# Making the seeds of the matrix Q on GpSimd alone, where VectorE made those of one channel half

## The chip, the cores and the metric

The kernel runs on one core of a Trainium2 chip. The metric is the device time of one execution, in microseconds. The core has five engines with an instruction queue each: TensorE (PE, matrix products), VectorE (DVE) and ScalarE (ACT) for elementwise work, GpSimd (POOL), and SyncE (SP), which issues transfers. Every queue is worked through in order, and the engines wait for each other by semaphores that the program names.

## The reference

It is one layer of a hybrid trunk over 2048 tokens of 1024 channels in float32. What matters here is the token mixer. Beside a gated short convolution it has a recurrence with one 64x64 state per head, for 16 heads:

```python
def step(state, inp):
    r_t, w_t, k_t, v_t, kk_t, a_t = inp
    sa = jnp.einsum('bhvk,bhk->bhv', state, kk_t)
    state = (state * w_t[:, :, None, :]
             - sa[..., None] * (kk_t * a_t)[:, :, None, :]
             + v_t[..., None] * k_t[:, :, None, :])
    y = jnp.einsum('bhvk,bhk->bhv', state, r_t)
    return state, y
...
merged = jax.nn.sigmoid(ga) * y_conv + jax.nn.sigmoid(gb) * y_rwkv
return merged @ w_out, v_first
```

After the mixer come a router and 32 experts of which each token uses two, and a last RMSNorm.

## The kernel before

The mixer is worked out in 32 steps. A step takes one tile of 128 channels (two heads, called the two halves; `HALF[0]` is partitions 0 to 63, `HALF[1]` is 64 to 127) and one group of 512 tokens, which is eight chunks of 64 tokens (`NC` = 8, `C` = 64). In a step the recurrence inside a chunk is turned into matrix products. They need the inverse of a triangular 64x64 matrix for each of the 16 pairs of chunk and head. The kernel builds it by doubling: two matrices `Tm` and `Qm` per pair start from a near-diagonal seed and are improved over five levels.

TensorE's order in a step is a projection part (`head` and `tail`: 64 products of 128x512 at L892 and some others), and then `inverse_and_recurrence`. That part goes by a list written out by hand, `SCHED`, which interleaves the products for the inverse of step i with the hops of the recurrence of step i-1 (`x`, `u` and `sy` for each chunk). It begins so:

```text
L, x0, LT (first half), u0, LT (second half), sy0, GK (first half), x1, GK (second half), u1,
Z1, sy1, TR0, T1, x2, Q1, u2, Z2, sy2, TR1, x3, T2, u3, Q2, sy3, ...
```

On TensorE `L` is L998, `LT` L1000, `GK` L1002, every `Z` L1004, every `T` L1006, every `Q` L1017, and every `TR` (a turn of `vt`, `Bb` or `Kb`) L986. The hops are L921 and L924 (x), L933 and L935 (u), L949 to L961 (sy) and L909 (the first part of the next x). All of them stand in one queue. In it T1 waits for the evacuation of Z1 (`Zm`) and for the semaphore `Q_seeded`, which says that the seeds of `Qm` are complete.

VectorE takes the results out of PSUM in the order of the same list: `Tm` from L (L1848), `LTb` from LT and `GKb` from GK in two operations each (L1837, `evacuate`), then `Zm` from Z (L1848), `Tm` and `Qm` from T and Q (L1851). Between them stand the state updates `St` (L1691). Behind the second evacuation of LT it calls `half_seeds`: two operations (L1858) that multiply one half of `LTb` with the mask `m0Ts` and write partitions 64 to 127 of `Qm`. Each covers 64 partitions by 4 chunks by 64 columns, 64x256.

GpSimd has six operations in a step (`seeds`): it adds the identity to `Tm` (L659), makes the seeds of partitions 0 to 63 of `Qm` in two operations of 64x256 (L663), waits for VectorE's two by the semaphore `Q_half`, adds the identity to all of `Qm` (L668) and tells TensorE by `Q_seeded`. Behind that it scales `Bb` and `Kb` in place (L653, `hat`). Those are read by the turns TR2 to TR5, in levels 3 to 5.

Of the kernel before, what the change touches and what calls it, by code (L numbers as in the profile page):

```python
# [9 lines left out]
ALU = mybir.AluOpType  # L10
# [14 lines left out]
HD = 64  # L25
# [58 lines left out]
def build(nc, io, out):  # L84
    ctx = ExitStack()
    with ctx:
# [3 lines left out]
        var_done gup_done bonus_done proj_done sg_ready a_ready carry_saved ksq_ready norm_max rk_ready  # L90
        rkbd_ready kk_ready b_ready ch_copied u_carry u_made cb_gated x_done u_done s_done y_done x_copied
        x_begun x_ahead yT_summed Q_near u_copied S_updated S_init yT_copied merged_ready merged_out gram_done
        gram_evac T_seeded Q_half Q_seeded tok_copied wo_in bcast_rows mix_done mixed x1_ready xn2_ready
        logit_done logit_copied aff_ready rank_mm hot_ready idx_mm idx_ready dest_ready blk_ready gu_done
        sig_ready silu_ready act_ready actT_done actT_ready y2_done y_dve y12 x2_ready o_ready shift_scaled
        shifted operands gates branch km_step rn_step P_step hats rs_step yc_step post_step conv_step sumsq
        ln_done rstd tr_done T_act T_dve index_col chain patterns ada_trip pair_go""".split()
        S = {n: ctx.enter_context(nc.semaphore(n)) for n in names}
        by_slot = "ada_w x_in mT_in x5_in x1_out xn2_out wi_in wo_e_in xg_in y_out".split()
        SL = {n: [ctx.enter_context(nc.semaphore(f"{n}{s}")) for s in range(2)] for n in by_slot}  # L100
# [6 lines left out]
        def sb(stack, name, shape, dt=F32):  # L107
            return stack.enter_context(nc.sbuf_tensor(name, shape, dt))
# [27 lines left out]
        m0Ts = sb(ctx, "m0Ts", [P, HD])  # L136
# [58 lines left out]
        LTb = [sb(p4, f"LTb{x}", [P, NC, 2 * HD]) for x in range(2)]  # L195
        GKb = [sb(p4, f"GKb{x}", [P, NC, 2 * HD]) for x in range(2)]
        Tm = sb(p4, "Tm", [P, NC, HD])
        Qm = [sb(p4, f"Qm{x}", [P, NC, HD]) for x in range(2)]
# [156 lines left out]
        evac_at = {u: n for n, u in enumerate(ON_DVE)}  # L355
        tok_at = {u: n for n, u in enumerate(ON_ACT)}
        NDV, NTK = len(ON_DVE), len(ON_ACT)

        def wait_gram(eng, i, u):

            eng.wait_ge(S["gram_done"], i * NUSE + use_at[u] + 1)

        def wait_evac(eng, i, u):

            if u in evac_at:
                eng.wait_ge(S["gram_evac"], i * NDV + evac_at[u] + 1)
            else:
                eng.wait_ge(S["tok_copied"], i * NTK + tok_at[u] + 1)
# [7 lines left out]
        HALF = (slice(0, 64), slice(64, 128))  # L376
# [254 lines left out]
        def _(pool):  # L631
# [15 lines left out]
            def over8(m):  # L647
                return m.unsqueeze(1).to_broadcast([P, NC, HD])

            def hat(i, p, M, n):  # L650
                pool.wait_ge(S["operands"], i * 5 + 2)
                pool.wait_ge(S["operands"], i * 5 + n)
                nc.gpsimd.tensor_tensor(M[:, :, :], M[:, :, :],  # L653
                                        pcs[p][:, :].unsqueeze(2).to_broadcast([P, NC, HD]), ALU.mult)\
                    .then_inc(S["hats"], 1)

            def seeds(i, p):
                wait_evac(pool, i, ("L", 0, 1, 0))
                nc.gpsimd.tensor_tensor(Tm[:, :, :], Tm[:, :, :], over8(idents[:, :]), ALU.add).then_inc(S["T_seeded"], 1)  # L659
                wait_evac(pool, i, ("LT", 0, 0, 0))  # L660
                pool.wait_ge(S["T_seeded"], i + 1)
                for a in range(2):
                    nc.gpsimd.tensor_tensor(Qm[p][HALF[0], 4 * a:4 * a + 4, :], LTb[p][HALF[a], 0:4, HD:2 * HD],  # L663
                                            m0Ts[HALF[a], :].unsqueeze(1).to_broadcast([HD, 4, HD]), ALU.mult)\
                        .then_inc(S["Q_near"], 1)
                    pool.wait_ge(S["Q_near"], i * 2 + a + 1)
                pool.wait_ge(S["Q_half"], i + 1)
                nc.gpsimd.tensor_tensor(Qm[p][:, :, :], Qm[p][:, :, :], over8(idents[:, :]), ALU.add)\  # L668
                    .then_inc(S["Q_seeded"], 1)
                hat(i, p, Bb, 4)  # L670
                wait_gram(pool, i, ("GK", 0, 1, 0))
                hat(i, p, Kb, 5)

            seeds(0, 0)
            seeds(1, 1)
            with pool.Fori(1, STEPS // 2) as h:
                seeds(h * 2, 0)
                seeds(h * 2 + 1, 1)
# [864 lines left out]
        def _(dve):  # L1543
            V = nc.vector
# [195 lines left out]
            def step(i, p):  # L1740
# [93 lines left out]
                def evacuate(kind, lv, b):  # L1834
                    u = (kind, lv, b, 0)
                    wait_gram(dve, i, u)
                    V.tensor_tensor((LTb if kind == "LT" else GKb)[p][:, 4 * b:4 * b + 4, :],  # L1837
                                    bank(u)[:, :].rearrange("p (c t) -> p c t", t=P),
                                    over(mN[:, :], 4), ALU.mult).then_inc(S["gram_evac"], 1)

                def evacuate_both(kind, lv):
                    u = (kind, lv, 1, 0)
                    wait_gram(dve, i, u)
                    bk = DUO[pair_of(u)][:, :, 0:4 * HD].rearrange("p b (c t) -> p b c t", t=HD)
                    to = {"L": Tm, "Z": Zm, "T": Tm, "Q": Qm[p]}[kind][:, :, :].rearrange("p (b c) t -> p b c t", b=2)
                    if kind in ("L", "Z"):
                        mask = m0s[:, :] if kind == "L" else mlevs[:, lv - 1, :]
                        ins = V.tensor_tensor(to, bk, mask.unsqueeze(1).unsqueeze(1).to_broadcast([P, 2, 4, HD]),  # L1848
                                              ALU.mult)
                    else:  # L1850
                        ins = V.tensor_tensor(to, to, bk, ALU.subtract)  # L1851
                    ins.then_inc(S["gram_evac"], 2)

                def half_seeds():

                    dve.wait_ge(S["gram_evac"], i * NDV + evac_at["LT", 0, 1, 0] + 1)
                    for a in range(2):
                        ins = V.tensor_tensor(Qm[p][HALF[1], 4 * a:4 * a + 4, :], LTb[p][HALF[a], 4:8, HD:2 * HD],  # L1858
                                              m0Ts[HALF[a], :].unsqueeze(1).to_broadcast([HD, 4, HD]), ALU.mult)
                    ins.then_inc(S["Q_half"], 1)  # L1860

                def hop(name, c):
                    if q is not None and name == "sy":
                        S_update(q, c, 1 - p)

                done = None
                for n, (what, name, *more) in enumerate(SCHED):
                    if what == "use" and name != "TR" and 1 in more[1]:
                        if name not in ("LT", "GK"):
                            evacuate_both(name, more[0])  # L1870
                        else:
                            evacuate(name, more[0], 0)
                            if SCHED[n + 1][0] == "hop":
                                hop(*SCHED[n + 1][1:])
                                done = n + 1
                            evacuate(name, more[0], 1)
                            if name == "LT":
                                half_seeds()
                    if what == "hop" and n != done:
                        hop(name, more[0])  # L1880
                if q is not None:
                    y_sum(q)

            step(0, 0)
            step(1, 1)
            with dve.Fori(1, STEPS // 2) as h:
                step(h * 2, 0)
                step(h * 2 + 1, 1)
# [258 lines left out]
```

## Time and profile before

| What | Value |
| --- | --- |
| median of 3 runs | 4946.42 us (4941.43 to 4950.04) |
| time of the profiled execution | 4945.55 us |
| its span, first to last instruction | 4943.8 us |
| granted TensorE clock, mean | 0.973 |
| TensorE busy | 4566.7 us, 92% |
| VectorE busy | 1631.0 us, 33% |
| ScalarE busy | 1346.4 us, 27% |
| GpSimd busy | 345.4 us, 7% |

The span is what the trace covers; the time is some 1.8 us longer and is what the runs are compared by. The mixer's 32 steps lie between about 200 us and 3080 us of the span.

### The profile page before, as it was taken

The page shows a single profiled execution, that of the slowest core. Times are in us where ns is not written, and L with a number is a line of the kernel's source. Part 1 is how long each engine was busy: PE and PEld are TensorE (multiplying, and loading weights), DVE is VectorE, ACT ScalarE, POOL GpSimd, SP SyncE. Part 2 cuts the span into 40 slices and gives each one's busy share as a digit, 9 for nine tenths or more (in the row PEclk, how much of TensorE's full clock was granted, in tenths as well). Part 3 has the DMA queues.
Part 4 walks back from the last instruction along what each step waited for, and adds up shares of the span by engine and source line. Part 5 has one row for each costly group of instructions (what it writes and reads, how often), then busy time and mean ns, then how long its engine had stood idle before and what let it go on. Part 6 is the DMA issues. An engine that isn't in the chain of part 4 may idle for free.

```text
span 4943.8 us, 91839 instructions
## 1 busy us (share of the span) xinstructions
PE 4566.7 (92%) x36823; PEld 2450.1 (50%) x36823; DVE 1631.0 (33%) x2946; ACT 1346.4 (27%) x3050; POOL 345.4 (7%) x466
## 2 busy tenths in 40 slices
PE   6999999999999999999999998994999999999992
PEld 4455555555555555555555555453444444444440
DVE  3334334334334334333343343224111111111115
ACT  4123333333333333333333333431111111111115
POOL 0001001001001000000010000000000000000004
PEclk8999999999999999999999999996999999999996
DMA  8101001001001001001001002333788888888887
GB/s 295 50 5 47 11 8 47 10 12 43 10 12 43 10 12 45 9 12 46 8 12 46 8 12 69 107 123 132 281 330 334 339 330 341 333 330 343 331 321 297
DMA packets 252914, 637.61 MB, mean 129 GB/s; under 512 B 11027, under 2 KB 96245, under 8 KB 252533
## 3 DMA queue, kind: packets, MB, share of 16 engines
q1 hardware_dynamic: 238852, 582.26, 32.3%
q0 software_dynamic: 13680, 49.81, 2.6%
q8 instruction: 295, 4.83, 0.4%
q14 instruction: 87, 0.70, 0.0%
HBM read 563.32 MB, written 68.71 MB: 128 GB/s over the span
## 4 chain that ended last, share of the span: by engine, by line
PE 87%; issue 4%; DVE 3%; DMA 2%; ACT 1%; SPq 1%; POOL 0%; DVEq 0%; POOLq 0%; ACTq 0%
PE bank L892 36%; PE bank L1218 18%; PE bank L1237 9%; PE bank L1106 5%; PE duo L1017 3%; PE duo L1004 2%; PE duo L1006 1%; PE duo L1207 1%; DMA yb<-y_s,dix 1%; PE bank L949 1%; ACT xs L1264 1%; PE bank L933 1%; PE duo L829 1%; PE duo L986 1%; PE bank L921 1%
## 5 line engine op out<-in xcount | busy, mean ns | idle before, releaser
L892 PE MATMUL bank<-hT,w 128*128 (+1 forms) x4096 | 1788.3, 593 | 0.0
L892 PEld LDWEIGHTS bank<-hT,w 128*128 128x128 f32 x4096 | 776.3, 190 | 991.0 <-issue 991.0
L1218 PE MATMUL bank<-WI,xT 128*128 128x512 f32 x2016 | 877.6, 593 | 2.4 <-DVE xT L2055 2.4
L1218 PEld LDWEIGHTS bank<-WI,xT 128*128 128x128 f32 x2016 | 378.9, 190 | 456.1 <-issue 456.1
L1237 PE MATMUL bank<-WO,aT 128*128 128x512 f32 x1008 | 443.1, 592 | 1.0 <-DVE ysb L2072 1.0
L1264 ACT ACT_TABLE_LOAD x268 | 343.8, 1283 | 21.1 <-DVE ub L1807 14.3
L2061 DVE TENSOR_TENSOR gsig<-bank,gsig 128x512 f32<-128x512 f32 x63 | 43.6, 692 | 847.4 <-ACT gsig L1264 847.4
L1237 PEld LDWEIGHTS bank<-WO,aT 128*128 128x128 f32 x1008 | 186.7, 190 | 212.6 <-issue 211.4
L1264 ACT ACTIVATE gsig<-bank 128x512 f32<-128x512 f32 x63 | 37.6, 597 | 827.6 <-PE bank L1218 827.6
L659 POOL TENSOR_TENSOR Tm<-Tm,idents 128x512 f32<-128x512 f32 x32 | 40.6, 1269 | 2826.3 <-DVE Tm L1848 2826.3
L1106 PE MATMUL bank<-wo,mT 128*128 128x512 f32 x512 | 233.6, 603 | 0.0
L1017 PE MATMUL duo<-Qm,Zm 64*64 64x64 f32 x5120 | 195.3, 225 | 16.5 <-issue 9.1
L1017 PEld LDWEIGHTS duo<-Qm,Zm 64*64 64x64 f32 x5120 | 176.4, 139 | 25.9 <-issue 21.9
L1264 ACT ACTIVATE T<-bank,par 128x512 f32<-128x512 f32 x96 | 66.0, 688 | 417.0 <-PE bank L892 417.0
L2072 DVE TENSOR_TENSOR ysb<-bank,g2b 128x512 f32<-128x512 f32 x126 | 81.2, 686 | 287.5 <-PE bank L1237 287.5
L1851 DVE TENSOR_TENSOR Qm<-Qm,duo 128x512 f32<-128x512 f32 x160 | 110.1, 688 | 191.0 <-PE duo L1017 191.0
L1264 ACT ACTIVATE xs<-bank 64x64 f32<-64x64 f32 x496 | 107.9, 218 | 145.2 <-PE bank L924 142.4
L1004 PE MATMUL duo<-Tm,LTb 64*64 64x64 f32 x5120 | 126.8, 225 | 21.0 <-issue 20.6
L1106 PEld LDWEIGHTS bank<-wo,mT 128*128 128x128 f32 x512 | 93.9, 191 | 101.1 <-issue 99.6
L1264 ACT ACTIVATE aT<-duo 128x512 f32<-128x512 f32 x63 | 37.6, 597 | 389.6 <-PE duo L1227 389.6
L1851 DVE TENSOR_TENSOR Tm<-Tm,duo 128x512 f32<-128x512 f32 x128 | 88.0, 688 | 155.2 <-PE duo L1006 155.2
L1264 ACT ACTIVATE ut<-bank 64x64 f32<-64x64 f32 x496 | 81.3, 212 | 184.6 <-PE bank L935 184.6
(340 smaller groups left out, 5369.0 us busy)
## 6 DMA issues: line engine op xcount, KB each, us to landing
WI<-in_w_expert_in_dram SPq DMA_DIRECT2D x63, 4096.0 KB, 17.2
WO<-in_w_expert_out_dram SPq DMA_DIRECT2D x63, 2048.0 KB, 7.9
w<-in_w_in_dram SPq DMA_DIRECT2D x64, 512.0 KB, 3.9
y_s<-ysb SPq DMA_DIRECT2D x63, 512.0 KB, 17.8
adaw<-in_w_ada_dram SPq DMA_DIRECT2D x12, 2048.0 KB, 12.9
xt<-in_x_dram SPq DMA_DIRECT2D x16, 512.0 KB, 9.0
WAc<-rank_s SPq DMA_DIRECT2D x32, 256.0 KB, 3.4
GDc<-rank_s SPq DMA_DIRECT2D x32, 256.0 KB, 3.2
```

Source lines behind the costliest of these rows:

```text
L829: mm(SB[:, :], UP[0:64, 0, :], WAc[0:64, :], start=True, stop=True).then_inc(S["zdec_done"], 1)
L892: ins = mm(PJ[j % 2][:, :], w[:, j, k, :], hT[:, k, ds(group(i) * G, G)], start=k == 0, stop=k == KT - 1)
L921: mm(xb[a][HALF[a], 0:HD], GKb[p][HALF[a], 4 * a + k, HD:2 * HD], tok[p][HALF[a], 0, 2 * k + a, :], start=True, stop=False)
L933: mm(xb[h][ha, 0:HD], Qm[p][HALF[h], slot_of(c), :], xsb[HALF[h], :], start=True, stop=False)
L1004: ins = mm(one, LTb[p][rows, e, HD:2 * HD], Tm[rows, e, :], start=True, stop=True)
L1017: ins = mm(bks[b][hp, k * HD:k * HD + HD], Zm[hp, c, :], Qm[p][hp, c, :], start=True, stop=True)
L1106: ins = mm(banks[2 * s + j][:, :], mT[:, s, k, :], wo[:, k, j * 512:j * 512 + 512], start=k == 0, stop=k == KT - 1)
L1218: ins = mm(GU[j][:, :], xT[:, s, k, :], WI[:, s, k, j * DE:j * DE + DE], start=k == 0, stop=k == KT - 1)
L1237: ins = mm(Y2[j][:, :], aT[:, s, k * P:k * P + P], WO[:, s, k, j * 512:j * 512 + 512], start=k == 0, stop=k == DE // P - 1)
L1264: return nc.scalar.activation(o, i, f, **kw)
L1851: ins = V.tensor_tensor(to, to, bk, ALU.subtract)
L2072: ins = V.tensor_tensor(ysb[:, s, 512 * j:512 * j + 512], banks[2 + j][:, :], g2b[:, 512 * j:512 * j + 512], ALU.mult)
```

## The change

VectorE's `half_seeds` is taken out, with its semaphore `Q_half`. GpSimd makes the seeds of both halves, in four operations of 64x256 one behind the other, and for the second half it waits for the second evacuation of LT. The operations are the same, and so are their operands. All else stays.

```diff
             def seeds(i, p):
                 wait_evac(pool, i, ("L", 0, 1, 0))
                 nc.gpsimd.tensor_tensor(Tm[:, :, :], Tm[:, :, :], over8(idents[:, :]), ALU.add).then_inc(S["T_seeded"], 1)
-                wait_evac(pool, i, ("LT", 0, 0, 0))
                 pool.wait_ge(S["T_seeded"], i + 1)
-                for a in range(2):
-                    nc.gpsimd.tensor_tensor(Qm[p][HALF[0], 4 * a:4 * a + 4, :], LTb[p][HALF[a], 0:4, HD:2 * HD],
-                                            m0Ts[HALF[a], :].unsqueeze(1).to_broadcast([HD, 4, HD]), ALU.mult)\
-                        .then_inc(S["Q_near"], 1)
-                    pool.wait_ge(S["Q_near"], i * 2 + a + 1)
-                pool.wait_ge(S["Q_half"], i + 1)
+                for h in range(2):
+                    wait_evac(pool, i, ("LT", 0, h, 0))
+                    for a in range(2):
+                        nc.gpsimd.tensor_tensor(Qm[p][HALF[h], 4 * a:4 * a + 4, :],
+                                                LTb[p][HALF[a], 4 * h:4 * h + 4, HD:2 * HD],
+                                                m0Ts[HALF[a], :].unsqueeze(1).to_broadcast([HD, 4, HD]), ALU.mult)\
+                            .then_inc(S["Q_near"], 1)
+                        pool.wait_ge(S["Q_near"], i * 4 + 2 * h + a + 1)
                 nc.gpsimd.tensor_tensor(Qm[p][:, :, :], Qm[p][:, :, :], over8(idents[:, :]), ALU.add)\
                     .then_inc(S["Q_seeded"], 1)
...
-                def half_seeds():
-
-                    dve.wait_ge(S["gram_evac"], i * NDV + evac_at["LT", 0, 1, 0] + 1)
-                    for a in range(2):
-                        ins = V.tensor_tensor(Qm[p][HALF[1], 4 * a:4 * a + 4, :], LTb[p][HALF[a], 4:8, HD:2 * HD],
-                                              m0Ts[HALF[a], :].unsqueeze(1).to_broadcast([HD, 4, HD]), ALU.mult)
-                    ins.then_inc(S["Q_half"], 1)
-
...
                             evacuate(name, more[0], 1)
-                            if name == "LT":
-                                half_seeds()
```

## Rows read from the trace of the kernel before

**Rows 1.** The page: busy time, its share and the instructions of each engine.

```profile
PE 4566.7 (92%) x36823; PEld 2450.1 (50%) x36823; DVE 1631.0 (33%) x2946; ACT 1346.4 (27%) x3050; POOL 345.4 (7%) x466
```

**Rows 2.** Stretches of one step: length, busy time (and count) of PE, PEld, DVE, ACT, POOL; clock.

```profile
1391.97:1399.60 7.63, 6.42 (x201) 5.26 (x201) 6.54 (x12) 2.27 (x12) 4.84 (x5) 1.00 0.01 2
1399.60:1424.00 24.40, 20.34 (x632) 17.23 (x632) 10.23 (x20) 8.63 (x37) 1.35 (x2) 1.00 0.01 4
1424.00:1483.50 59.50, 59.49 (x140) 26.14 (x138) 19.19 (x34) 19.06 (x25) 0.00 (x0) 1.00 0.05 14
```

**Rows 3.** Timeline of the same step, TensorE: start, length, instructions, idle before.

```profile
1396.00 0.65 PE L1002 MATMUL duo<-AR,Kb 64*64 64x128 f32 x14
...
1397.08 0.69 PE L1004 MATMUL duo<-Tm,LTb 64*64 64x64 f32 x32
...
1398.30 0.28 PE L961 MATMUL bank<-AR,St 64*64 64x64 f32 x2
1399.00 0.41 PE L986 MATMUL duo<-ident,vt 128*128 128x128 f32 x2 [0.42 <-DVE GKb L1837]
1399.60 0.69 PE L1006 MATMUL duo<-Zm,Qm 64*64 64x64 f32 x32 [0.19 <-DVE Zm L1848]
```

**Rows 4.** Timeline of the same step, VectorE.

```profile
1395.52 0.69 DVE L1837 TENSOR_TENSOR LTb<-duo,mN 128x512 f32<-128x512 f32 x1
1396.24 1.29 DVE L1858 TENSOR_TENSOR Qm<-LTb,m0Ts 64x256 f32<-64x256 f32 x2
1397.57 1.29 DVE L1837 TENSOR_TENSOR GKb<-duo,mN 128x512 f32<-128x512 f32 x2
1398.77 0.68 DVE L1848 TENSOR_TENSOR Zm<-duo,mlevs 128x512 f32<-128x512 f32 x1
```

**Rows 5.** Timeline of the same step, GpSimd.

```profile
1395.52 1.73 POOL L663 TENSOR_TENSOR Qm<-LTb,m0Ts 64x256 f32<-64x256 f32 x2 [0.31 <-DVE LTb L1837]
1397.68 1.27 POOL L668 TENSOR_TENSOR Qm<-Qm,idents 128x512 f32<-128x512 f32 x1 [0.43 <-DVE Qm L1858]
1398.90 1.05 POOL L653 TENSOR_TENSOR Bb<-Bb,pcs 128x512 f32<-128x512 f32 x1
```

**Rows 6.** Timeline of the same step, the four seed operations one by one.

```profile
1395.52 0.73 POOL L663 TENSOR_TENSOR Qm<-LTb,m0Ts 64x256 f32<-64x256 f32 x1 [0.31 <-DVE LTb L1837]
1396.32 0.93 POOL L663 TENSOR_TENSOR Qm<-LTb,m0Ts 64x256 f32<-64x256 f32 x1
...
1396.24 0.42 DVE L1858 TENSOR_TENSOR Qm<-LTb,m0Ts 64x256 f32<-64x256 f32 x1
1396.68 0.86 DVE L1858 TENSOR_TENSOR Qm<-LTb,m0Ts 64x256 f32<-64x256 f32 x1
```

**Rows 7.** GpSimd's seeds over the whole run: durations in ns, least, median and longest.

```profile
L663 POOL TENSOR_TENSOR Qm<-LTb,m0Ts x64: 722/762/947, 216.8 to 3048.0; 64x256 f32<-64x256 f32 x64
```

**Rows 8.** Timeline of the first step, GpSimd and TensorE.

```profile
216.79 1.59 POOL L663 TENSOR_TENSOR Qm<-LTb,m0Ts 64x256 f32<-64x256 f32 x2
218.47 1.27 POOL L668 TENSOR_TENSOR Qm<-Qm,idents 128x512 f32<-128x512 f32 x1
...
219.87 0.53 PE L1006 MATMUL duo<-Zm,Qm 64*64 64x64 f32 x21 [0.19 <-POOL Qm L668]
```

**Rows 9.** Timeline of the last step, GpSimd and TensorE.

```profile
3049.27 1.26 POOL L668 TENSOR_TENSOR Qm<-Qm,idents 128x512 f32<-128x512 f32 x1 [0.43 <-DVE Qm L1858]
...
3052.64 0.69 PE L1002 MATMUL duo<-AR,Kb 64*64 64x128 f32 x3 [4.44 <-issue]
...
3055.95 1.13 PE L1006 MATMUL duo<-Zm,Qm 64*64 64x64 f32 x32
```

**Rows 10.** Waits of TensorE in 28 steps: in total, times, longest.

```profile
PE duo L1004 <- issue: 18.7, 25, 1.0
PE bank L935 <- issue: 14.4, 14, 1.3
...
PE duo L1006 <- issue: 8.2, 17, 0.7
...
PE duo L1017 <- issue: 5.7, 12, 0.9
```

**Rows 11.** Timeline of TensorE: Q1 in three steps of these twelve.

```profile
395.17 0.33 PE L1017 MATMUL duo<-Qm,Zm 64*64 64x64 f32 x4 [0.94 <-issue]
...
577.94 0.97 PE L1017 MATMUL duo<-Qm,Zm 64*64 64x64 f32 x26 [0.32 <-issue]
...
2779.19 0.62 PE L1017 MATMUL duo<-Qm,Zm 64*64 64x64 f32 x14 [0.68 <-issue]
```

More of the change, by code:

```diff
@@ L92, in build @@
         x_begun x_ahead yT_summed Q_near u_copied S_updated S_init yT_copied merged_ready merged_out gram_done
[L93 to L97, printed above, removed]
+        gram_evac T_seeded Q_seeded tok_copied wo_in bcast_rows mix_done mixed x1_ready xn2_ready logit_done
+        logit_copied aff_ready rank_mm hot_ready idx_mm idx_ready dest_ready blk_ready gu_done sig_ready
+        silu_ready act_ready actT_done actT_ready y2_done y_dve y12 x2_ready o_ready shift_scaled shifted
+        operands gates branch km_step rn_step P_step hats rs_step yc_step post_step conv_step sumsq ln_done
+        rstd tr_done T_act T_dve index_col chain patterns ada_trip pair_go""".split()
         S = {n: ctx.enter_context(nc.semaphore(n)) for n in names}
```

## The prediction

> **What bounds the kernel now.** I read the page first: TensorE is busy 92% of the span, VectorE 33%, GpSimd 7% [rows 1]. This says only that TensorE's queue sets the time. The busy time of another engine counts for nothing by itself; what counts is where TensorE waits for it. So next I read the stretches of one step, the one that begins near 1392 us (the 14th of 32). The reader is to see that TensorE has no slack in 59.50 us of it, 59.49 busy. Its idle time lies in the part that this change touches, 1.2 us of 7.63, and in the 24.40 us behind it [rows 2]. The change is made in VectorE's and GpSimd's queues, so its price in a step is how far it moves the first thing that TensorE waits for. TensorE doesn't catch up later: behind T1 everything stands in one queue, and the products of the inverse feed on each other.
>
> TensorE's timeline shows two such waits. TR0 waits 0.42 us for the evacuation of GK, and T1 starts at 1399.60, 0.15 after the end of `Zm` (1398.77 + 0.68 = 1399.45) [rows 3, 4]. The second condition of T1, the complete seeds of `Qm`, is met at 1397.68 + 1.27 = 1398.95 [rows 5]. It has 0.50 us of slack. So VectorE's chain ends last before T1, and GpSimd's chain is right behind it.
>
> **What the change removes.** VectorE loses two operations of 64x256, from 1396.24 to 1397.53. They are followed by GKb at 1397.57 and Zm at 1398.77 [rows 4]. Without them GKb can start when the product GK ends, 1396.65 [rows 3], and some 0.1 us for the signal, say 1396.75. Two evacuations of 1.29 us end at 1398.04. Zm comes behind both them and the product Z1 (ends 1397.77 [rows 3]); I let it start at 1398.0 and end at 1398.7. So `Zm` is 0.75 us earlier. TR0 starts as soon as the queue is through with sy1, whose last products end at 1398.58 [rows 3]. T1 starts 0.60 behind TR0 [rows 3], so TensorE could then have T1 at about 1399.1 to 1399.2, 0.4 to 0.5 us sooner. Removal alone would be a gain of 0.4 to 0.5 us a step.
>
> **What it adds.** GpSimd gets two more operations of 64x256 in front of the identity. The first of the present two runs beside a VectorE evacuation and takes 0.73; the second starts 0.80 after the first and takes 0.93, because it lies beside VectorE's seeds, which are 0.42 and then 0.86 long [rows 6]. The two engines stretch each other there: each has one short and one long operation, and the short ones are the free durations. With VectorE's seeds gone, what runs beside GpSimd's are evacuations from PSUM. Those cost it nothing in the rows: the first seed beside LTb takes 0.73, and the identity beside GKb takes the 1.27 that it takes in the first step too [rows 5, 6, 8]. So I take 0.73 for all four, which is also near the least of all 64 (722 ns) [rows 7], and 0.80 from start to start.
>
> The Trainium skill bears on this (SBUF — State Buffer, section "SBUF: two separate sides"): a VectorE operation with two SBUF inputs and a GpSimd operation that reads SBUF take a shared pair of ports in turns, each for a whole instruction. This case's trace agrees, with 0.86 against 0.42. By this rule the second to fourth seed take 0.73; without it one might leave them at 0.93, and the term below would be 0.6 us larger in a step.
>
> The chain in the step near 1392 us is then: seeds at 1395.52, 1396.32, 1397.12 and 1397.92; the second evacuation of LT ends at 1396.21 [rows 4], so the third seed doesn't wait. Identity at 1398.72, done at 1398.72 + 1.27 = 1399.99. That is 1.04 later than before. T1 starts 0.13 to 0.15 behind what it waits for (0.13 behind GpSimd in the first step: 218.47 + 1.27 = 219.74, T1 at 219.87 [rows 8]), so at 1400.14 instead of 1399.60: **0.54 us later in a step.** VectorE's gain falls into this wait: `Zm` is ready at 1398.7 and nothing reads it.
>
> Bounds of this term: if each of the last three seeds took 0.93 (the longest row 0.947 [rows 7]), it would be 0.54 + 0.6 = 1.14. If 0.722, 0.51. I take 0.54, by the operation with the same neighbour.
>
> The Trainium skill also speaks against the direction of the change (GPSIMD Engine Reference, section 4.1 "Engine selection"): a two-input elementwise operation is to go to VectorE, as GpSimd takes about twice as long. By the rows it is 0.73 to 0.42, 1.7 times. With a factor of two, an estimate by that page, each of the seeds would take 0.84 and T1 would come about 0.4 us later still.
>
> What else is queued behind the later identity: the two operations on Bb and Kb, 1.05 us each [rows 5], now done at about 1402.1 instead of 1400.95. The first turn that reads Bb stands in level 3, TR2, behind T2, Q2 and Z3 in the list, several us later. They cost nothing while that cover lasts. Behind T1 on TensorE stand x2, Q1, u2 and all the rest; ScalarE and VectorE wait for their results, so all of it moves with T1. No transfer is moved.
>
> **The sum over steps.** In 29 steps, the second to the thirtieth, T1 is 0.54 later: 15.7 us. The thirty-first, the first behind TensorE's loop, I round up to 0.6. The first step has no recurrence in between, and its T1 waits for GpSimd already [rows 8]: 216.79 + 4 x 0.80 + 1.27 + 0.13 = 221.4, against 219.87, 1.5 us later. In the last step TensorE stands for 4.44 us in the middle of GK and reaches T1 at 3055.95, 5 us after the identity [rows 9]: 0. Together 17.8 us.
>
> **What takes part of it back.** TensorE's queue also halts with no semaphore behind it ("issue"), always in front of the same instruction of the loop body. In 28 steps Q1 has such a halt in twelve, 5.7 us together [rows 10]. Seven of them are 0.32 to 0.33, the others 0.59, 0.60, 0.68, 0.68 and 0.94; three of the twelve are shown [rows 11]. With the halt of 0.32 the queue goes on at the same distance from the start of the step each time, and steps without it are there at 8.2 us already. I read that as instructions that arrive at their own time. A halt 1 us behind T1, whose end doesn't hang on T1, swallows a delay of T1 up to its own length: 7 x 0.32 + 5 x 0.54 = 4.9 us. The later halts (Z, T, u: 18.7, 14.4 and part of the 8.2 us [rows 10]) keep, I think, their distance from T1, as the instructions that ask for the next ones come behind T1 as well. Net: 17.8 - 4.9 = **12.9 us slower**. From the profiled execution's own 4945.55 this is 4958.5; that execution is 0.9 below the median of the runs, so against 4946.42 it is 4959.3 us.
>
> **Rivals.**
> *The full delay.* The halts before Q1 move along: 17.8 us, 4964. For it: it takes only that fetching also waits for T1. Against it: the fixed distance. 0.22.
> *The delay is swallowed.* T1's wait lets the instruction queue run ahead, so that the later halts shrink too. They are worth 18.7 + 14.4 + 8.2 = 41 us [rows 10]; if a tenth to a third of it goes, 4 to 13 us, the result is 0 to 9 us slower, some 4951. For it: they vary between steps from nothing to over 1 us. Against it: most come over 10 us behind T1. 0.26.
> *The other side: faster.* The same mechanism with its price larger: it decides when more than 23 of the 41 us vanish, as 12.9 must be paid first and 9.9 gained. At 30 of 41 it gives 4929. GpSimd being quicker can't do it: a gain at T1 needs the identity done before 1399.45, so seeds at 0.66 us from start to start, where no row is below 0.72 for the work alone. 0.05.
> *Slower by more.* The seeds stay at 0.93 without VectorE beside them: 1.14 a step, about 34 + 2 less some 6 of halts, 30 us, 4976. 0.07.
>
> **How the numbers follow.** The likeliest case has 0.40 and the numbers 4954 to 4963. About 0.2% (9.9 us) is what a measurement of this kernel can tell from no change. Slower by over that: 0.07 and 0.22 and three quarters of 0.40, with something of the swallowed case: 0.62. Within it: the rest of the likeliest case and most of the swallowed one, 0.32. Faster 0.06. The range is 4947 to 4969: it leaves out the faster case, the lower end of the swallowed one and the seeds at 0.93.
>
> **What would show it.** In the profile after, L663 has 128 operations with a mean near 0.73 us, and L1858's are gone. GKb starts 0.8 us sooner, Zm ends 0.7 sooner. The idle time in front of T1 is 0.6 to 1.0 us a step, put down to the identity on GpSimd (some 20 to 30 us in all), and that in front of TR0 goes. Q1's halts fall from 5.7 us to about 1. I am wrong if GpSimd's seeds are longer than 0.8 with no VectorE seeds beside them, if T1's delay is other than 0.54, or if the issue halts of the later products change by over 8 us.

## The result and the profile after

The changed kernel takes 4956.65 us (median of 13 runs, 4952.1 to 4965.1). The kernel before takes 4946.42 in the runs beside it (13 runs, 4934.19 to 4953.4). The ratio is 1.0023, with a 95% interval of 1.0015 to 1.0032. A second comparison on another occasion gave 1.0026 (1.0015 to 1.0038). So the change makes the kernel 10 to 13 us slower, where 12.9 was forecast.

The profiled execution took 4961.41 us, 4.8 above its median, and the one shown of before 0.9 below its own. So the difference of the two spans (15.9 us) is more than the change is worth. The page after, its first row and the row of GpSimd's seeds, answers to [rows 1] and [rows 7]:

```profile
PE 4574.5 (92%) x36823; PEld 2464.0 (50%) x36823; DVE 1591.6 (32%) x2882; ACT 1347.3 (27%) x3050; POOL 384.3 (8%) x530
```

```profile
L664 POOL TENSOR_TENSOR Qm<-LTb,m0Ts x128: 717/724/735, 218.8 to 3065.2; 64x256 f32<-64x256 f32 x128
```

VectorE has 64 operations less and GpSimd 64 more. None of GpSimd's seeds is long any more: 717 to 735 ns, where the durations before ran up to 947.

Then the timeline of the same step as before, the 14th. The first product of L starts at 1400.77 here and at 1392.32 before; places in a step are counted from there in all that follows. These rows answer to [rows 3 to 6]:

```profile
1403.89 1.53 POOL L664 TENSOR_TENSOR Qm<-LTb,m0Ts 64x256 f32<-64x256 f32 x2 [0.24 <-DVE LTb L1838]
1405.58 1.53 POOL L664 TENSOR_TENSOR Qm<-LTb,m0Ts 64x256 f32<-64x256 f32 x2 [0.16 <-POOL Qm L664]
1407.18 1.26 POOL L669 TENSOR_TENSOR Qm<-Qm,idents 128x512 f32<-128x512 f32 x1
...
1405.16 1.29 DVE L1838 TENSOR_TENSOR GKb<-duo,mN 128x512 f32<-128x512 f32 x2 [0.49 <-PE duo L1003]
1406.38 0.69 DVE L1849 TENSOR_TENSOR Zm<-duo,mlevs 128x512 f32<-128x512 f32 x1
...
1406.96 0.44 PE L987 MATMUL duo<-ident,vt 128*128 128x128 f32 x2
1408.54 0.69 PE L1007 MATMUL duo<-Zm,Qm 64*64 64x64 f32 x32 [1.14 <-issue]
```

The reader is to see three things. `Zm` is ready at 6.30 (1406.38 + 0.69), 0.83 us sooner than before, and TR0 starts at 6.19 without a wait. Nothing comes of either, because the identity on GpSimd ends at 7.67 and T1 starts at 7.77, before at 7.28. And TensorE stands for 1.14 us in front of T1. The trace puts that down to "issue", that is to nothing it can name, although GpSimd's identity ends 0.10 us before T1 starts. In some runs below the same wait is put down to GpSimd: in e3 in 20 of 28 steps, and in e10 and e11, where other products stand between T1's two waits. One has to compare the times, not read the name alone.

The waits of TensorE in the 28 steps of [rows 10], after:

```profile
PE duo L1007 <- issue: 36.5, 47, 1.1
...
PE duo L1005 <- issue: 13.9, 26, 1.0
PE bank L936 <- issue: 11.7, 14, 1.3
...
PE duo L1018 <- issue: 1.6, 4, 0.4
```

L1007 is every T product. The 28 waits in front of T1 are 30.8 of its 36.5 us; before, 2.6 us stood in front of T1. The halts in front of Q1 (L1018) went from 5.7 us in twelve steps to 1.6 in four.

### The profile page after: what moved, and what is told of

The parts are those of the page before. It is cut to its first block, busy times and chain, and to the rows that moved or that the text cites. A ratio compares the mean times of both kernels' runs of the same rounds, so it can differ in the third digit from the quotient of the medians.

```text
span 4959.7 us, 91869 instructions
## 1 busy us (share of the span) xinstructions
PE 4574.5 (92%) x36823; PEld 2464.0 (50%) x36823; DVE 1591.6 (32%) x2882; ACT 1347.3 (27%) x3050; POOL 384.3 (8%) x530
## 4 chain that ended last, share of the span: by engine, by line
PE 89%; issue 4%; DMA 2%; DVE 2%; ACT 2%; SPq 1%; POOL 1%; DVEq 0%; POOLq 0%; ACTq 0%
PE bank L893 36%; PE bank L1219 17%; PE bank L1238 9%; PE bank L1107 5%; PE duo L1018 4%; PE duo L1005 2%; PE duo L1007 1%; PE duo L1208 1%; ACT xs L1265 1%; PE bank L950 1%; PE bank L934 1%; PE duo L987 1%; DMA yb<-y_s,dix 1%; PE duo L830 1%; PE bank L936 1%
## 5 line engine op out<-in xcount | busy, mean ns | idle before, releaser
L1018 PE MATMUL duo<-Qm,Zm 64*64 64x64 f32 x5120 | 202.5, 231 | 14.5 <-ACT tok L1265 7.2
L1018 PEld LDWEIGHTS duo<-Qm,Zm 64*64 64x64 f32 x5120 | 183.7, 144 | 23.3 <-issue 19.1
L1007 PE MATMUL duo<-Zm,Qm 64*64 64x64 f32 x4096 | 105.7, 231 | 43.3 <-issue 39.2
L1005 PE MATMUL duo<-Tm,LTb 64*64 64x64 f32 x5120 | 130.8, 228 | 15.4 <-issue 14.9
## 6 DMA issues: line engine op xcount, KB each, us to landing
WI<-in_w_expert_in_dram SPq DMA_DIRECT2D x63, 4096.0 KB, 17.1
```

Source lines behind the costliest of these rows:

```text
L1005: ins = mm(one, LTb[p][rows, e, HD:2 * HD], Tm[rows, e, :], start=True, stop=True)
L1007: ins = mm(one, Qm[p][rows, slot_of(c), :], Zm[rows, slot_of(c), :], start=True, stop=True)
L1018: ins = mm(bks[b][hp, k * HD:k * HD + HD], Zm[hp, c, :], Qm[p][hp, c, :], start=True, stop=True)
```

## The experiments

Every ratio is to the kernel before, from runs on the same chip. Theory A is the prediction's: GpSimd's chain sets the place of T1, T1's delay is carried to the end of the step, and only halts whose end doesn't hang on T1 swallow a part. Rivals are named in the expectations.

**What a comparison can tell (e9).** The kernel before against itself.

> The kernel before once more, under a name of its own: a ratio of 1.000 within 0.0012, which shows what the comparison can tell. Its profile is a second sample of TensorE's clock and of the instruction halts. Theory D (the changed kernel's idle time in front of T1 makes the clock fall behind it): again no fall in the first 3 us behind T1, some 8 to 12 elsewhere. If falls are as many here as in the two profiles of the changed kernel (15 and 12 in 28 steps), they do not carry its loss.

Measured 1.0000 (0.9990 to 1.0009). Its profile gives a second sample of the halts before the change:

```profile
PE duo L1004 <- issue: 18.5, 27, 1.1
PE bank L935 <- issue: 11.7, 14, 1.3
...
PE duo L1017 <- issue: 10.1, 14, 1.0
PE duo L1006 <- issue: 8.4, 19, 0.7
```

Q1's halts are 10.1 us here and 5.7 in the first profile. A single execution gives such a sum only to within some 4 us. The places of T1 (7.28) and of `Zm` are the same to 0.01 us.

Both profiles also show what the halts called "issue" are. The profile lists transfers of 16 KB on a queue of the kind "instruction", 295 of them in the whole run. Q1 has its halts only in every second of the 28 steps, and there one of these transfers lies shortly in front of it, as in front of the halt that ends at 577.94 [rows 11]:

```profile
q8 instruction: 1, 0.02, 3.0%
```

This is the stretch from 575 to 577 us of the first profile; the transfer ends at 576.44, and no other begins between 571.9 and 579.5. Of the halts of more than 0.25 us, all 66 in the 28 steps of the first profile, all 68 of the second and, the wait of T1 left out, 50 of 51 in the changed kernel end 1.15 to 1.65 us behind the end of such a transfer, though these come only every 4 us or so. I take them for waits for instructions from here on. In the steps of this kind the transfer in front of Q1 ends at 7.3 and 7.6 us of the step (medians, as are those that follow, in the two profiles), and at 7.4 to 7.5 in the runs e2, changed and e1, where T1 starts at 6.65, 7.77 and 8.59. It doesn't depend on T1. The next transfer does: in the other steps it ends at 10.1 and 10.5 before, at 9.4 in e2, at 11.2 and 11.3 in the two profiles of the changed kernel and at 12.0 in e1.

**The suspected cost made larger (e1).**

```diff
+                nc.gpsimd.tensor_tensor(Qm[p][HALF[1], 4:8, :], LTb[p][HALF[1], 4:8, HD:2 * HD],
+                                        m0Ts[HALF[1], :].unsqueeze(1).to_broadcast([HD, 4, HD]), ALU.mult)\
+                    .then_inc(S["Q_fifth"], 1)
+                pool.wait_ge(S["Q_fifth"], i + 1)
```

> The changed kernel with one of GpSimd's four seed operations made a second time before the identity, so five of 64x256 in a row; the result is the same. Theory A (GpSimd's chain sets T1, and a delay of T1 is carried to the end of the step): T1 another 0.80 us later in a step, 30 x 0.80 = 24 us on top of the changed kernel's 10, less the 1.6 us of halts that its Q1 still has: 30 to 34 us over the kernel before, ratio 1.0060 to 1.0069. Theory B (delays of T1 are mostly swallowed by the instruction halts behind it): 15 to 22 us over it, ratio 1.003 to 1.0045. Theory C (the loss of the changed kernel has another cause than T1's wait for GpSimd): T1 does not move, ratio as the changed kernel's 1.0023.

Measured 1.0082 (1.0069 to 1.0096), about 40 us. One seed is made a second time, and the identity waits for it. The timeline of the 14th step (L at 1416.52):

```profile
1422.95 0.72 POOL L669 TENSOR_TENSOR Qm<-LTb,m0Ts 64x256 f32<-64x256 f32 x1
1423.75 1.26 POOL L673 TENSOR_TENSOR Qm<-Qm,idents 128x512 f32<-128x512 f32 x1
...
1425.11 0.62 PE L1011 MATMUL duo<-Zm,Qm 64*64 64x64 f32 x26 [1.95 <-issue]
```

T1 starts at 8.59, 0.82 later than in the changed kernel, as expected. Times 30 that is 24.6 us, and the time grew by some 28 over the changed kernel (1.0082 against 1.0023 and 1.0026). Theory C is out, as T1 moved, and the ratio is far above theory B's range. It is above theory A's too, and its parts don't come apart cleanly. The mean clock of TensorE is 0.9662 over the six runs against 0.9709 in the 27 of the kernel before. Within the runs of one and the same kernel, 196 in all, a mean clock lower by 0.001 goes with 3.0 us more time. By that estimate some 14 of the 28 us go with the clock, and only 14 would be left for the delay. The lengths of the steps say more: the 28 steps last 2607.0 us together, against 2577.8 and 2584.3 in the two profiles of the changed kernel. T1's place is 22.7 us of the difference. From T1 to the next projection a step needs 24.45 us on average, against 24.25 and 24.51. So the delay shows in full in the length of the step, and what lies behind T1 stays as long in sum. That halts there hide a part of it, which the lower clock then costs again, isn't excluded.

**VectorE's part taken out, nothing put in (e2).** The near-diagonal part of the seeds is left out.

```diff
-                for h in range(2):
+                for h in range(1):
...
-                nc.gpsimd.tensor_tensor(Qm[p][:, :, :], Qm[p][:, :, :], over8(idents[:, :]), ALU.add)\
+                nc.gpsimd.tensor_tensor(Qm[p][:, :, :], over8(idents[:, :]), over8(idents[:, :]), ALU.mult)\
```

> VectorE's part removed and nothing put in its place: GpSimd makes the two seeds of the first half as before, and the last operation of the same size writes the identity over them, so the near-diagonal part of the seeds of Q is left out of the computation. GpSimd's chain then ends before Zm. Both theories let T1 start right behind TR0, at 6.8 to 6.9 us from the first product of L instead of 7.28, 0.4 to 0.5 us sooner. Theory A1 (the halt in front of Q1 ends at its own time in every second step, whatever T1 does): half of the steps gain nothing, 14 to 15 steps x 0.45 = 6 to 7 us faster than the kernel before, ratio 0.9985 to 0.9988, and the halts of Q1 grow from 5.7 us to about 12. Theory B (the halts move with T1): 12 to 14 us faster, ratio 0.9972 to 0.9976, halts of Q1 unchanged.

Measured 0.9982 (0.9971 to 0.9994), 9 us faster. The 14th step (L at 1396.69) and the halts of Q1 (L1019) in 28 steps:

```profile
1402.89 0.44 PE L988 MATMUL duo<-ident,vt 128*128 128x128 f32 x2
1403.25 0.69 PE L1008 MATMUL duo<-Zm,Qm 64*64 64x64 f32 x32
```

```profile
PE duo L1019 <- issue: 17.1, 14, 1.7
```

T1 starts at 6.56, 0.72 sooner, more than expected: it needn't keep 0.6 us from TR0, it follows at 0.36. Thirty times that is over 20 us, and only 9 arrived. The rest is in Q1's halts, 17.1 us in every second step. From T1 to the first product of the next projection, the first, third and so on of these steps need 25.29 us on average and the others 24.22, against 24.70 and 24.15 in the kernel before (starts of T1 and of the next L892 product in the timelines). In the first kind Q1 has its halt; T1 is 0.63 sooner there and 0.59 is given back. The others, the 14th step among them, gain 0.72 and keep nearly all of it. That is theory A1: the halt in front of Q1 ends at its own time, at 8.5 to 9.3 us of the step here and at 8.5 to 9.2 in the two profiles of before. The ratio alone lies between the ranges of A1 and B and would not decide; the halts do.

**VectorE's operations put back without a purpose (e3).** They write to `Zm`, which is overwritten afterwards.

```diff
+                    for a in range(2):
+                        ins = V.tensor_tensor(Zm[HALF[1], 4 * a:4 * a + 4, :], LTb[p][HALF[a], 4:8, HD:2 * HD],
+                                              m0Ts[HALF[a], :].unsqueeze(1).to_broadcast([HD, 4, HD]), ALU.mult)
```

> The changed kernel, with VectorE's two seed operations put back in their old place but writing to a matrix that is overwritten later, so they serve nothing. Theory A (only GpSimd's chain counts, and the two engines stretch each other's operations with two SBUF inputs): GpSimd's second or third seed becomes 0.9 instead of 0.72, T1 0.2 to 0.4 us later than in the changed kernel, Zm 0.7 us later without any effect; 4 to 10 us over the changed kernel, 14 to 20 over the one before, ratio 1.003 to 1.004. Rival (VectorE's chain matters too, what it was relieved of gave something back in the changed kernel): 15 us and more over the changed kernel, ratio 1.005 and more. If the operations don't disturb each other: as the changed kernel, 1.0023.

Measured 1.0029 (1.0020 to 1.0039).

```profile
1408.15 1.81 POOL L664 TENSOR_TENSOR Qm<-LTb,m0Ts 64x256 f32<-64x256 f32 x2 [0.24 <-DVE LTb L1838]
1410.12 1.52 POOL L664 TENSOR_TENSOR Qm<-LTb,m0Ts 64x256 f32<-64x256 f32 x2 [0.16 <-POOL Qm L664]
...
1413.10 1.13 PE L1007 MATMUL duo<-Zm,Qm 64*64 64x64 f32 x32 [0.97 <-POOL Qm L669]
```

GpSimd's first pair takes 1.81 instead of 1.53, the second is untouched. T1 is at 8.07 in this step and at 8.00 on average. Zm is as late as in the kernel before, and that costs nothing, because GpSimd ends later still. The ratio lies just under theory A's range, 2 to 3 us over the changed kernel where T1's place, 0.23 later in 30 steps, is worth 7; the intervals allow both. The rival's 15 us are out. So what VectorE was relieved of brought the changed kernel nothing that can be measured.

**All four on VectorE (e12).**

```diff
+                    for h in range(2):
+                        for a in range(2):
+                            ins = V.tensor_tensor(Qm[p][HALF[h], 4 * a:4 * a + 4, :],
+                                                  LTb[p][HALF[a], 4 * h:4 * h + 4, HD:2 * HD],
+                                                  m0Ts[HALF[a], :].unsqueeze(1).to_broadcast([HD, 4, HD]), ALU.mult)
```

> The mirror of the change: VectorE makes all four seed operations behind the second evacuation of LT, GpSimd only adds the identities; the result is the same. Without GpSimd's seeds beside them VectorE's take 0.42 each: 3.9 to 5.65 us, GKb to 6.95, Zm done at 7.55, T1 at 7.7 (7.28 in the kernel before, 7.77 in the changed one). GpSimd's identity is done at 7.0 and isn't in the way. Theory A (T1's place gives the time, whichever chain ends last): 30 x 0.4 = 12 us, less what the halts of every second step swallow, 5 to 10 us slower than before, ratio 1.001 to 1.002. Rival (VectorE has time to spare, 33% busy, so that its operations cost nothing): 1.000.

Measured 1.0007 (0.9998 to 1.0017). The 14th step, L at 1401.50:

```profile
1405.43 1.72 DVE L1853 TENSOR_TENSOR Qm<-LTb,m0Ts 64x256 f32<-64x256 f32 x4
1407.18 1.29 DVE L1831 TENSOR_TENSOR GKb<-duo,mN 128x512 f32<-128x512 f32 x2
1408.39 0.68 DVE L1842 TENSOR_TENSOR Zm<-duo,mlevs 128x512 f32<-128x512 f32 x1
...
1408.62 0.41 PE L980 MATMUL duo<-ident,vt 128*128 128x128 f32 x2 [0.85 <-DVE GKb L1831]
1409.22 0.69 PE L1000 MATMUL duo<-Zm,Qm 64*64 64x64 f32 x32 [0.19 <-DVE Zm L1842]
```

The chain came as worked out: four seeds in 1.72 us, T1 at 7.72. Yet it costs 3 to 4 us, where the changed kernel with T1 only 0.06 later costs 10 to 13. Theory A's range, 1.001 to 1.002, is missed, and the rival's 1.000 lies in the interval. So T1's place alone doesn't give the time. The halts of Q1 are down to 1.5 us in both. I can't say what makes the rest; the idle time stands in two pieces here (0.85 and 0.19) and in one there. The profiles show two differences that might carry it. The clock falls behind T1 in 2 of 28 steps here and in 8 and 6 in the changed kernel. And the halts of the later T products are 2.9 us together here, against 5.6 and 9.7 there and 8.2 before. Neither was tested, and the mean clock is that of the kernel before beside it (0.9712 and 0.9713).

**Three on GpSimd, one on VectorE (e4).**

```diff
-                for a in range(2):
...
+                for n, (h, a) in enumerate(((0, 0), (0, 1), (1, 1))):
...
-                    for a in range(2):
+                    for a in range(1):
                         ins = V.tensor_tensor(Qm[p][HALF[1], 4 * a:4 * a + 4, :], LTb[p][HALF[a], 4:8, HD:2 * HD],
```

> GpSimd makes three of the four seed operations and VectorE one, both in the place of the kernel before; the result is the same. GpSimd: seeds at 3.2, 4.0 and 4.9 us, the identity at 5.7 to 5.8, done at 7.0; VectorE is 0.86 us shorter, Zm done at 6.6. Theory A: T1 at 7.1 to 7.2 instead of 7.28, 0.1 to 0.2 us sooner a step, and half of it lost in the halts of every second step: 1 to 4 us faster than the kernel before, ratio 0.9992 to 0.9998, which can hardly be told from none. Rival (one engine at a time is better, handing over costs more than the operations): 3 us and more slower, ratio over 1.0006.

Measured 0.9991 (0.9982 to 0.9999), L at 1395.36:

```profile
1398.56 1.73 POOL L665 TENSOR_TENSOR Qm<-LTb,m0Ts 64x256 f32<-64x256 f32 x2 [0.32 <-DVE LTb L1840]
1400.45 0.73 POOL L665 TENSOR_TENSOR Qm<-LTb,m0Ts 64x256 f32<-64x256 f32 x1 [0.16 <-DVE GKb L1840]
1401.26 1.27 POOL L671 TENSOR_TENSOR Qm<-Qm,idents 128x512 f32<-128x512 f32 x1
...
1402.62 0.69 PE L1009 MATMUL duo<-Zm,Qm 64*64 64x64 f32 x32 [0.64 <-issue]
```

The one seed left on VectorE still stretches GpSimd's second (1.73 for the pair), so the identity ends at 7.17 and T1 stands at 7.27, where it stood before. The expected 0.1 to 0.2 us sooner didn't come. The ratio is at the edge of what can be told from 1, and T1's place gives no reason for a gain, so I don't count it as one.

**x2 in front of T1 (e7 and e8).** One swap in the order by hand, in the changed kernel and in the one with three and one.

```diff
-    plan += level(1, [n[5], None, n[6], n[7]])
+    plan += level(1, [n[5], n[6], None, n[7]])
```

> The changed kernel with one swap in the order by hand: the hop x2 stands in front of T1 instead of behind it, on every engine. In the changed kernel its state update is done at 6.5 us from the first product of L, so x2 can run inside T1's wait. T1 stays at 7.77 and Q1 comes 0.26 us sooner behind it, u2 isn't late. Theory A: 30 x 0.26 = 8 us less than the changed kernel, less what the halts take: ratio 1.0005 to 1.0015. Theory D adds that the idle stretch in front of T1 is cut in two of some 0.2 and 0.6 us and that the falls of the clock there become fewer: ratio 0.9990 to 1.0005.

> Three seed operations on GpSimd and one on VectorE, with x2 in front of T1. With three and one, T1 stood at 7.27 behind an idle time of 0.6 us. Now x2 fills that: T1 at 7.3, Q1 0.26 us sooner. Theory A: about 7 us less than three and one alone, less the halts of every second step: ratio 0.9978 to 0.9990. Theory D: few falls of the clock behind T1, ratio 0.9970 to 0.9985. If x2 holds up T1, because its state update comes later than 6.6 us: T1 at 7.5 or later and a ratio of 1.000.

Measured 1.0016 (1.0004 to 1.0027) and 1.0014 (1.0004 to 1.0024). T1 stood at 7.78 and 7.27 as expected. The first is just above theory A's range, 5 us less than the changed kernel run beside it, which the two intervals do not tell apart. Q1's halts are back at 8.1 us there, so part of the 0.26 us was swallowed. From T1 to the next projection a step needs 24.53 us, no less than in the changed kernel (24.25 and 24.51). The second was expected at 0.9990 or below and is worse than three and one without the swap. Both theories fail there: from T1 to the projection it needs 24.84 us, against 24.70 with three and one alone, though x2 no longer stands between T1 and Q1. I have no shown reason.

**TensorE kept busy in the wait (e5, e6, e10, e11).** In front of T1, between the evacuation of Zm and the wait for `Q_seeded`, products are made that nobody reads: two of 128x512, one of 128x512, or two of 128x64.

```diff
                     if (kind, lv) == ("T", 1):
+                        for _ in range(2):
+                            mm(SB[:, :], ident[:, :], run[:, :], start=True, stop=True)
                         pe.wait_ge(S["Q_seeded"], i + 1)
```

> The changed kernel once more, beside the next three on the same chip: 1.0015 to 1.0032 against the kernel before. Its profile is a second sample of where TensorE's clock falls to its lower level. In the first profile that was 10 times in the first microseconds behind T1 (7.5 to 9.4 us from the first product of L), in the profile of the kernel before never. Theory D (the idle time of 1.1 us in front of T1 brings these falls): 6 to 14 of them again. Theory A (only the delay counts, the falls are chance): few, at other places.

> The changed kernel, but TensorE makes two products of 128x512 that nobody reads (into the bank that T1 overwrites) between the evacuation of Zm and its wait for the seeds of Q. T1 can't start earlier, so its delay stays at 0.49 us; its idle time of 1.1 us goes down to 0.2 to 0.3. Theory D (a part of the loss is the lower clock behind an idle wait: a step with such a fall lasts 1.3 to 1.9 us longer): no falls at 7.5 to 9.5 us any more, 8 to 12 us less than the changed kernel, ratio to the kernel before 0.9995 to 1.0008. Theory A (the delay alone costs 10 us): ratio as the changed kernel's, 1.002 or more, since two products are added.

> The changed kernel with one product of 128x512 that nobody reads in T1's wait, where the run before had two. The trace of two showed that each goes through TensorE as two instructions of 0.43 us, so that two pushed T1 to 8.29; one takes 0.86 us and ends before the seeds do. T1 at 7.77, idle time in front of it 0.2 us. Theory D: no fall of the clock right behind T1; if the falls there carried part of the loss and nothing takes their place, 1.0005 to 1.0015 against the kernel before. Theory F (the longer code moves the places at which TensorE runs out of instructions; with two products the halts in front of the Z products rose from 14 to 53 us): two pairs of instructions more shift them half as far, halts of Z at 20 to 40 us, ratio 1.003 to 1.006. Pure theory A: as the changed kernel, 1.0025.

> The changed kernel with two products of 128x64 in T1's wait: as many instructions more as with the two of 128x512 (four pairs), but only 0.2 us of work inside 1.1 us of idle time, so T1 stays at 7.77. Theory F: the halts of the Z products rise to about 50 us as there, and the ratio to the kernel before is 1.005 to 1.008 although nothing in front of T1 has changed. Theory A with the halts as a mere by-product: halts and ratio as the changed kernel's, 1.002 to 1.003.

The clock first. In the changed kernel the row of a stretch right behind T1 (T1 at 2606.50) shows half the clock, 1.2 instead of 2.4 GHz. The stretch in front of it is idle. The products of T1 take 1.13 us there instead of 0.69:

```profile
2605.50:2606.50 1.00, 0.00 (x0) 0.03 (x1) 0.00 (x0) 0.38 (x1) 1.00 (x2) 0.98 0.00 0
2606.50:2609.90 3.40, 3.40 (x90) 3.40 (x91) 0.76 (x2) 0.44 (x2) 1.90 (x2) 0.50 0.02 5
```

```profile
2606.50 1.13 PE L1007 MATMUL duo<-Zm,Qm 64*64 64x64 f32 x32 [1.10 <-issue]
```

With one such window laid over T1 in each of 28 steps, a lower clock shows in 8 of them in the changed kernel and in 6 in its second profile (e5). It shows in 0 and 2 in the two profiles of the kernel before, and in 12 with the fifth seed. (The ten of the expectation of e5 count the first two steps as well.) From T1 to the projection, seven steps of the changed kernel with such a fall need 25.3 us on average, and seven of the same kind without one 23.4. Three of the seven have a second fall later; the four with one alone need 24.6. That looked like a cause of the loss. All falls in the 28 steps are 8 and 7 in the two profiles of before and 15 and 12 in those of the changed kernel. So the count in e9, which was to acquit the clock if it was as high as in the changed kernel, doesn't do so, and the profiles don't show that the falls behind T1 take the place of others (8 and 5 stand elsewhere before, 7 and 6 after). But the profiled executions aren't typical: both of before have a mean clock of 0.973 and 0.974, over the 0.971 of the runs, and those of the changed kernel 0.969 and 0.970. The means over all runs say otherwise: the granted clock is 0.9709 in the eight runs of the changed kernel and 0.9705 in the 24 runs of the kernel before beside them. The difference is known to about 0.0011, so at 3.0 us for 0.001 the clock carries at most some 2 us of the loss. Only with the fifth seed is the mean clearly lower.

The fillers show that the place of the falls can be changed without a gain. With one product of 128x512 the idle time is 0.33 us, and no fall comes in the first microseconds behind T1 in any of 28 steps, but there are 13 later ones. The kernel didn't get faster: 1.0035 (1.0022 to 1.0047), 1.0085 (1.0072 to 1.0098) with two, which also push T1 to 8.29, and 1.0058 (1.0046 to 1.0071) with the two small ones, T1 at 7.82. The waits of TensorE with the small ones:

```profile
PE duo L1005 <- issue: 48.0, 43, 1.8
PE duo L1007 <- POOL Qm L669: 22.2, 28, 0.8
PE bank L925 <- issue: 11.8, 14, 1.2
```

and with one large one:

```profile
PE duo L1005 <- issue: 33.1, 31, 1.7
PE bank L934 <- issue: 19.3, 17, 1.7
```

The halts of the Z products (L1005) are 48.0 us, against 13.9 and 18.4 in the two profiles of the changed kernel, with nothing else changed than four pairs of short instructions in a wait. Theory F holds as far as it was tested, with halts and ratio inside its ranges in both runs: where in the code TensorE waits for instructions, and how long, depends on what stands in the loop. Whether the number of instructions does it or their place in front of the wait wasn't told apart. It is a cost of its own, and with four pairs larger than that of the change studied.

## Why the prediction was right

*GpSimd's chain.* The identity was to be done at 1.04 us later than before; it ended at 7.67 against 6.64, 1.04 later before rounding. The seeds without VectorE's beside them took 0.72 (0.73 said). Between the second and third stands a wait, 0.89 from start to start instead of 0.80, and the first started 0.08 sooner; the two cancel.

*T1.* 0.54 us later was said, 0.49 came: T1 starts 0.10 behind the identity, not 0.14. In the first step 1.4 us (1.5 said). In the last it was 10.5 us into the step where it was 12.0 before; this step has a long halt of its own in both. In the second profile of the changed kernel it is 12.0 again.

*VectorE's gain.* Zm was to be ready at 1398.7, 6.4 into the step, and is at 6.30. It is worth nothing, as e3 shows. My estimate of what the removal alone would bring, 0.4 to 0.5 us at T1, was too low: e2 shows 0.72.

*The sum.* With 0.49 in 29 steps, 1.4 in the first and 0.6 in the thirty-first it is 29 x 0.49 + 1.4 + 0.6 = 16.2 us instead of 17.8. The halts were to swallow 4.9. Q1's fell from 5.7 and 10.1 us in two profiles of before to 1.6 and 1.5, so by 4 to 9. That leaves 7 to 12; 10 to 13 were measured. The mechanism is supported from both sides, by e2 (T1 sooner, half the gain lost in Q1's halts) and e1 (T1 still later, Q1's halts used up, the delay in full in the length of the step). It isn't closed. The 28 steps lasted 2568.6 and 2567.5 us before and 2577.8 and 2584.3 after. T1's place is 13.8 and 14.0 of that; behind T1 the first pair of profiles gives 5 us back, as worked out, and the second adds 3. And e12 has nearly the same T1 and costs some 8 us less. That the net of the two terms came out inside what was measured owes something to luck: the first was taken 1.6 us too large, and the second is known only to some 5 us either way.

*The signs of being wrong.* T1's delay was 0.49 and not 0.54. The later halts (Z, T and u, the wait of T1 left out) were not to change by over 8 us. They are 41.3 and 38.6 us in the two profiles of before and 31.3 and 41.0 in those of the changed kernel: 10 less in the first, the same in the second. That they keep their distance from T1 fits the transfers of instructions that move with it, but their sum isn't shown to stay. The idle time in front of T1 was to be 0.6 to 1.0 us, put down to GpSimd; it is 1.14 and was called "issue".

*The rivals.* The full delay is out by the fall of Q1's halts; the time speaks against it less, as 16 us lie inside the interval of the second comparison. The swallowed delay is out as the whole story, by the length of the steps, most clearly in e1; that later halts swallow some microseconds isn't excluded. Seeds that stay at 0.93 are out. The faster case named halts as its mechanism. They can indeed move the time by more than the change does, but it takes a change of TensorE's code (e10, e11), and there is none here.

*What I hadn't in it.* The fall of TensorE's clock behind a wait of 1.1 us. It didn't change the result by more than some 2 us, as far as the means can tell.

## What to carry to other kernels

When two engines feed one wait, work out where each chain ends before moving work between them. The one with 7% load had 0.50 us of slack at the only place that counts, and four operations of 0.8 us did not fit where two did. Ask also whose operations are beside each other: a GpSimd operation of 0.72 us took 0.93 beside a VectorE operation that reads two matrices from SBUF. And when TensorE runs through its code in short products, look for halts for instructions: the one in front of Q1 swallowed part of a gain in e2 and of the loss in the changed kernel, and a few short instructions more in the loop cost 0.3%. Don't trust such a difference between kernels with different TensorE code before the halts have been compared.

## What the runs showed of the hardware that was not expected

- Halts of TensorE that the trace calls "issue" end 1.15 to 1.65 us behind the end of a 16 KB transfer of instructions, in 66 of 66 and 68 of 68 halts of over 0.25 us.
- The halt in front of Q1 ends at its own time, whatever T1 does: T1 0.7 us sooner lengthened these halts from 5.7 and 10.1 us to 17.1, T1 0.5 us later cut them to 1.6. The transfers behind it move with T1.
- Four pairs of short instructions more in TensorE's loop body raised the halts in front of one line from 14 to 18 us up to 48.0, and the time by some 16 us over the changed kernel (1.0058 against 1.0023 and 1.0026).
- Behind 1.1 us of idle time the granted clock fell to 1.2 GHz in 8 and 6 of 28 steps, behind 1.9 us in 12; with 0.33 us in none. The mean clock over the runs was the same with 1.1 us as without (0.9709 and 0.9705).
- A product of 128x512 in float32 that was meant as one instruction goes through TensorE as two, 0.43 us from start to start.
